# Branch and output stage of a hybrid encoder layer joined into one block, with the first output inputs split in the last branch tile

## What is computed

```python
y_gla  = o.astype(x.dtype) @ gla_wo                 # 512 -> 1024
y_pool = (pooled * jax.nn.silu(pool_z)) @ pool_wo
y_gdn  = o.astype(x.dtype) @ gdn_wo
gts = jax.nn.sigmoid(gates.astype(f32)).reshape(B, L, N_BRANCH, D_MODEL)
merged = gts[:, :, 0] * y_gla + gts[:, :, 1] * y_pool + gts[:, :, 2] * y_gdn
y = merged.astype(x.dtype) @ w_out
x = x + rmsnorm(y, norm_post)
```

## Time and profile before

| | us |
|---|---|
| median of three runs | 2622.28 |
| profiled execution | 2621.7 |
| span of the profiled execution (first to last instruction) | 2619.9 |
| PE busy | 2499.7 (95%) |
| DVE busy | 1036.3 (40%) |
| POOL busy | 808.8 (31%) |
| ACT busy | 675.5 (26%) |

### The profile page before, as it was taken

One profiled execution on the slowest core, in us unless ns is written; L12 is line 12 of the kernel. 1 busy time (PEld: TensorE's weight loads), 2 busy tenths in 40 slices (PEclk: granted clock), 3 DMA queues, 4 the chain that ended last, 5 costly groups with the idle time before them and its releaser, 6 DMA issues. The chain is left out here.

```text
span 2619.9 us, 40153 instructions
## 1 busy us (share of the span) xinstructions
PE 2499.7 (95%) x15943; PEld 2396.5 (91%) x15943; DVE 1036.3 (40%) x1603; ACT 675.5 (26%) x1350; POOL 808.8 (31%) x711
## 2 busy tenths in 40 slices
PE   5899999999999998998999999999999979997998
PEld 4799999999988898998999999999999879997886
DVE  6510011222455654002555555455555443323332
ACT  7111111111145431111232223222332243212222
POOL 1111121111111111114465456454555214332222
PEclk9899999999999999998999999999999879999999
DMA  5112412100111121242223324443224355543343
GB/s 159 47 66 107 193 63 74 66 33 33 66 50 49 49 74 68 74 136 68 82 76 111 111 81 127 159 122 97 81 78 108 119 174 179 198 162 140 114 145 106
DMA packets 200143, 264.95 MB, mean 101 GB/s; under 512 B 16176, under 2 KB 175296, under 8 KB 194432
## 3 DMA queue, kind: packets, MB, share of 16 engines
q1 hardware_dynamic: 200064, 263.86, 31.2%
HBM read 164.54 MB, written 99.29 MB: 101 GB/s over the span
## 5 line engine op out<-in xcount | busy, mean ns | idle before, releaser
L178 POOL TENSOR_TENSOR w_hi<-w_raw,zero 128x1024 fp32r<-128x1024 f32 x77 | 146.9, 1908 | 1243.0 <-PE dense L426 943.3
L424 PE MATMUL dense<-h_hi_first,w_hi 128*128 128x352 f32 x1080 | 355.2, 329 | 15.5 <-ACT row_y L671 8.4
L425 PE MATMUL dense<-h_lo_first,w_hi 128*128 128x352 f32 x1080 | 352.2, 326 | 0.0
L426 PE MATMUL dense<-h_hi_first,w_lo 128*128 128x352 f32 x1080 | 351.7, 326 | 0.0
L425 PE MATMUL dense<-h_lo_second,w_hi 128*128 128x352 f32 x1080 | 349.8, 324 | 0.0
L426 PE MATMUL dense<-h_hi_second,w_lo 128*128 128x352 f32 x1080 | 348.7, 323 | 0.0
L424 PE MATMUL dense<-h_hi_second,w_hi 128*128 128x352 f32 x1080 | 347.7, 322 | 0.0
L1314 PE MATMUL gate_bank<-h_hi_first,w_hi 128*128 128x352 f32 x768 | 274.4, 357 | 5.1 <-SPq L1232 4.4
L1314 PE MATMUL gate_bank<-h_hi_first,w_lo 128*128 128x352 f32 x768 | 249.5, 325 | 0.0
L1314 PE MATMUL gate_bank<-h_lo_first,w_hi 128*128 128x352 f32 x768 | 249.3, 325 | 0.0
L424 PEld LDWEIGHTS dense<-h_hi_first,w_hi 128*128 128x128 f32 x1080 | 206.1, 191 | 19.9 <-ACT row_y L671 8.7
(11 more groups left out here) (212 smaller groups left out, 4625.4 us busy)
## 6 DMA issues: line engine op xcount, KB each, us to landing
w_raw<-in_w_in SPq DMA_DIRECT2D x77, 512.0 KB, 5.8
rows_then_inputs<-scratch_feat SPq DMA_DIRECT2D x16, 1856.0 KB, 9.2
scratch_feat<-row_y SPq DMA_DIRECT2D x28, 1056.0 KB, 4.9
gate<-scratch_gates SPq DMA_DIRECT2D x12, 2112.0 KB, 8.7
scratch_gates<-gate_row SPq DMA_DIRECT2D x96, 176.0 KB, 1.9
o_raw<-scratch_branch_out SPq DMA_DIRECT2D x6, 2112.0 KB, 12.9
scratch_merged<-merged SPq DMA_DIRECT2D x48, 176.0 KB, 1.8
rows_then_inputs<-in_x_prompt SPq DMA_DIRECT2D x16, 512.0 KB, 3.7
```

Source lines behind the costliest of these rows:

```text
L178: nc.gpsimd.tensor_tensor(self.hi[:, p], raw, zeros, ALU.add).then_inc(self.high_ready, 1)
L424: nc.tensor.matmul(out, w_hi[:, p, k], h_hi[:, k, cols], start=(k == 0), stop=False)
L425: nc.tensor.matmul(out, w_hi[:, p, k], h_lo[:, k, cols], start=False, stop=False)
L426: mm = nc.tensor.matmul(out, w_lo[:, p, k], h_hi[:, k, cols], start=False, stop=(k == KD - 1))
```

## The change

`branch_phase` and `output_phase` become one function, `closing_phase`, with one block. What each engine did in the output stage follows in its queue directly on what it did in the branch stage, without the clearing of semaphores and the barrier between them. What is computed is the same, with the same operations.

Buffers: since the buffers of both stages don't fit side by side, those of the output stage lie over ones of the branch stage. The split w_out, the split and the raw merged tiles, x, the scaled result and so on are placed over `wo_hi` and `wo_lo`, over the gates (half 0) and over the ring and `o_raw` of `LateWeights`. `block_under(row)` tells which block m of wo must be through on PE before a row of 4096 bytes may be written. In PSUM the even token tiles have two banks of their own, `y_tok`, and the odd ones take two banks of the first buffer of `y`.

Order: in the last branch tile, SP loads the last row of w_out behind the store of block 3, waits for the stores 0 to 3 of that tile to land and loads merged 0 and 1; the gain is loaded behind the store of block 7, then x 0 and 1 when PE is through with the branch stage. ACT, behind the last gates, loads the table and makes the high rows of w_out and then those of merged 0 and 1, each when its block of wo is through: blocks 0, 1, 1, 2, 3, 3, 4, 5 for the rows, 5 and 6 for merged. DVE makes the low rows between its products: row 0 behind product 1, rows 1 and 2 behind product 2, row 3 behind 3, rows 4 and 5 behind 4, row 6 behind 5, row 7 and merged 0 behind 6, merged 1 behind 7. PE goes on from the last branch block to the first token tile.

```diff
...
+        w_hi = over("wout_hi", hi_at, [P, KD, DM], F32R)
+        w_lo = over("wout_lo", lo_at, [P, KD, DM], F32R)
+        m_hi = over("m_hi", hi_at + KD * ROW, [P, 2, KD, P], F32R)
+        m_lo = over("m_lo", lo_at + KD * ROW, [P, 2, KD, P], F32R)
+        x_in = over("x_again", hi_at + (KD + 2) * ROW, [P, 2, DM])
+        normed = over("normed", lo_at + (KD + 2) * ROW, [P, 2, DM])
+        w_last = over("wout_last", late.gate_at, [P, DM])
+        m_raw = over("m_raw", late.gate_at + ROW, [P, 2, KD, P])
+        gain = over("post_gain", late.ring_at, [P, DM])
+        squares = over("y_squares", late.ring_at + ROW, [P, DM])
+        result = over("result", late.o_at, [P, 2, DM])
...
+        y_tok = ctx.enter_context(nc.psum_tensor("y_tok", [P, DM], F32))
...
+        def tokens_bank(p):
+            return y[:, 0, 0:2, :].rearrange("p a b -> p (a b)") if p else y_tok
...
+        def block_under(row):
+            return ((row + 1) * ROW - 1) // (4 * K * P)
...
+                    sp.dma_start(y_out, result[0:n, p]).then_inc(stored[p], 16)
                 tile(0, first=True)
                 sp.wait_ge(wo_split, KD)
                 late.load_first(sp, d)
-                with sp.Fori(1, TILES_B - 1) as t:
+                with sp.Fori(1, LAST) as t:
                     tile(t)
                 sp.wait_ge(o_split, TILES_B * 3)
                 late.load_then(sp, d)
-                tile(TILES_B - 1, ahead=False)
+                for m in range(KD):
+                    store_merged(LAST, m)
+                    if m == 3:
+                        sp.dma_start(w_last[:, :], d["w_out"][(KD - 1) * P:KD * P, :]).then_inc(w_last_landed, 16)
+                        for q in range(2):
+                            sp.wait_ge(merged_stored[q], 16 * (4 * LAST + 2))
+                        load_m(0, 0)
+                        load_m(1, 1)
+                sp.wait_ge(w_split, late.FIRST)
+                sp.dma_start(gain[:, :], d["norm_post"].to_broadcast([P, DM])).then_inc(gain_landed, 16)
+                sp.wait_ge(y_ready, TILES_B * KD)
+                load_x(0, 0)
+                load_x(1, 1)
                 for q in range(2):
                     sp.wait_ge(merged_stored[q], 16 * 4 * TILES_B)
+                with sp.Fori(0, CHUNKS // 2 - 1) as i:
+                    for p in range(2):
+                        load_next_m(i * 2 + (p + 2), p)
+                        store(i * 2 + p, p)
+                        load_x(i * 2 + (p + 2), p)
+                load_next_m(CHUNKS, 0, NS_)
+                store(CHUNKS - 2, 0)
+                load_x(CHUNKS, 0, NS_)
+                store(CHUNKS - 1, 1)
+                store(CHUNKS, 0, NS_)
+                sp.wait_ge(stored[0], 16 * (CHUNKS // 2 + 1))
...
+                def w_row(k):
+                    act.wait_ge(y_ready, LAST * KD + block_under(k) + 1)
+                    if k == 0:
+                        act.wait_ge(late.first_landed, 16)
+                    if k == late.FIRST:
+                        act.wait_ge(late.then_landed, 16)
+                    if k == KD - 1:
+                        act.wait_ge(w_last_landed, 16)
+                    nc.scalar.copy(w_hi[:, k], w_raw(k)).then_inc(w_high, 1)
+                def high(t, i, p, n):
+                    act.wait_ge(m_landed[p], i * 16 + 16)
+                    if isinstance(t, int) and t < 2:
+                        act.wait_ge(y_ready, LAST * KD + block_under(KD + t) + 1)
+                    else:
+                        act.wait_ge(tok_ready, t - 1)
+                    nc.scalar.copy(m_hi[:, p, :, 0:n], m_raw[:, p, :, 0:n]).then_inc(m_high, 1)
...
+                    open_gates(LAST, half)
+                use_log_exp_tables(nc)
+                for k in range(KD):
+                    w_row(k)
+                act.wait_ge(eps_set, 1)
+                high(0, 0, 0, P)
+                high(1, 0, 1, P)
+                for p in range(2):
+                    statistics(p, p, P)
+                    high(p + 2, 1, p, P)
+                with act.Fori(1, CHUNKS // 2 - 1) as i:
+                    for p in range(2):
+                        statistics(i * 2 + p, p, P)
...
+                def token_tile(t, p, n):
+                    pe.wait_ge(m_split, t + 1)
+                    if isinstance(t, int) and t == 1:
+                        pe.wait_ge(y_gated, TILES_B * KD - 1)
+                    elif not (isinstance(t, int) and t < 2):
+                        pe.wait_ge(normed_ready, t - 1)
+                    for half in range(2):
+                        cols = slice(half * 512, half * 512 + 512)
+                        out = tokens_bank(p)[0:n, cols]
+                        for k in range(KD):
+                            if isinstance(t, int) and t == 0 and half == 0:
+                                pe.wait_ge(w_split, k + 1)
+                            nc.tensor.matmul(out, m_hi[:, p, k, 0:n], w_hi[:, k, cols], start=(k == 0), stop=False)
+                            nc.tensor.matmul(out, m_hi[:, p, k, 0:n], w_lo[:, k, cols], start=False, stop=False)
+                            mm = nc.tensor.matmul(out, m_lo[:, p, k, 0:n], w_hi[:, k, cols], start=False,
+                                                  stop=(k == KD - 1))
+                    mm.then_inc(tok_ready, 1)
                 tile(0, first=True)
                 with pe.Fori(1, TILES_B) as t:
                     tile(t)
+                token_tile(0, 0, P)
+                token_tile(1, 1, P)
+                token_tile(2, 0, P)
+                token_tile(3, 1, P)
+                with pe.Fori(1, CHUNKS // 4) as i:
+                    for u in range(4):
+                        token_tile(i * 4 + u, u % 2, P)
...
+                for m in range(KD):
+                    gated(LAST, m)
+                    for k in range(KD):
+                        if block_under(k) == m - 1:
+                            w_row_low(k)
+                    if block_under(KD) == m - 1:
+                        m_low(0, 0, P)
+                m_low(1, 1, P)
+                dve.wait_ge(gain_landed, 16)
+                norm(0, 0, P)
+                m_low(2, 0, P)
+                norm(1, 1, P)
+                m_low(3, 1, P)
+                with dve.Fori(1, CHUNKS // 2 - 1) as i:
+                    for p in range(2):
+                        norm(i * 2 + p, p, P)
+                        m_low(i * 2 + (p + 2), p, P)
+                norm(CHUNKS - 2, 0, P)
...
```

More of the change, by code:

```diff
@@ L1925, in store, with tile @@
                         .then_inc(merged_stored[m % 2], 16)
-                def tile(t, ahead=True, first=False):
+                def tile(t, first=False):
                     if first:
@@ L2051, in _ @@
-                low(0, 0)
-                weights_low(0)
-                low(0, 1)
-                low(0, 2)
-                weights_low(1)
-                for m in range(KD - 1):
-                    if m + 2 < KD:
-                        weights_low(m + 2)
-                    gated(0, m, first=True)
-                low(1, 0)
-                low(1, 1)
-                gated(0, KD - 1)
-                low(1, 2)
-                with dve.Fori(1, TILES_B - 1) as t:
-                    tile(t)
@@ L2066, in _ @@
-                tile(TILES_B - 1, ahead=False)
-            @block.gpsimd
-            def _(pool):
-                def tile(t, first=False):
-                    for m in range(KD):
-                        q = m % 2
-                        pool.wait_ge(y_gated, t * KD + (m + 1))
-                        nc.gpsimd.tensor_tensor(part[:, q], prod[:, q, 0], prod[:, q, 1],
-                                                ALU.add).then_inc(part_ready, 1)
-                        pool.wait_ge(part_ready, t * KD + (m + 1))
-                        if not (first and m < 2):
-                            pool.wait_ge(merged_stored[q], t * (4 * 16) + (m // 2) * 16)
-                        nc.gpsimd.tensor_tensor(merged[:, q], part[:, q], prod[:, q, 2],
-                                                ALU.add).then_inc(merged_ready, 1)
-                tile(0, first=True)
-                with pool.Fori(1, TILES_B) as t:
-                    tile(t)
@@ L2298, in _, with tile, token_tile @@
             def _(pool):
-                def tile(t, i, p, n):
+                def tile(t, first=False):
+                    for m in range(KD):
+                        q = m % 2
+                        pool.wait_ge(y_gated, t * KD + (m + 1))
+                        nc.gpsimd.tensor_tensor(part[:, q], prod[:, q, 0], prod[:, q, 1],
+                                                ALU.add).then_inc(part_ready, 1)
+                        pool.wait_ge(part_ready, t * KD + (m + 1))
+                        if not (first and m < 2):
+                            pool.wait_ge(merged_stored[q], t * (4 * 16) + (m // 2) * 16)
+                        nc.gpsimd.tensor_tensor(merged[:, q], part[:, q], prod[:, q, 2],
```

(12 more changed lines are left out.)

289 lines of the change are left out of this document (102 added, 187 removed).

## The result

The changed kernel takes **2604.78 us** (median of four runs, 2602.7 to 2609.2) where the kernel before took 2622.01 in runs beside it: a ratio of 0.9936 with a 95% interval of 0.9919 to 0.9954. A second series of five runs gave 2603.79 (2602.6 to 2604.4) against 2620.73, a ratio of 0.9933 (0.9919 to 0.9946). The forecast was 2605.2 with a range of 2603.0 to 2609.5. The profiled execution took 2605.52 with a span of 2603.7 (forecast 2604.6 and 2602.8).

The account below looks back on a forecast made before the run. PE was taken to bound both stages, with one hole between them. Removing 17.57 us and adding a 0.45 us wait gave 17.1 us less, from a median of 2622.28 to 2605.2 us, range 2603.0 to 2609.5.

Parts of the forecast that it names:

- The hole: Between branch and output stage: PE's idle time and the stretched first token tile go, next tile starting 17.57 us earlier.
- The new wait: Last branch tile, before block 4: PE waits for product 2, queued behind low row 0; +0.45 us, bounds zero and 2.4.
- The cover at the end of the last tile: Merged 0's low part done at 2405.0, wanted by PE at 2406.93: 1.9 us cover, cost nothing, upper bound 2.1 us.
- Rival 1: First token tile: lock or late landing delays merged 0's low part; 0.8 to 2.1 us, 2606 to 2609; chance 0.10.
- The next tiles: Later token tiles: merged 2 issued near 2413.6, split by about 2424, wanted at 2428.7; cover 4.7 us, cost nothing.
- rivals 2 and 4: Third token tile's inputs late, 2608.8, chance 0.04; merged loads delaying every third tile, level or slower (2627.7), chance 0.08.
- The tail: End of the kernel: clearing more semaphores taken at nothing, bounds nothing and 0.95 us.
- Rival 3: ACT and DVE order keeps the split behind the branch stage; some 10 us of gain left, 2612; chance 0.02.
- The other signs: Around the boundary: last product near 2407.1, squares near 2418.0, clock 1.00 between 2400 and 2435, no first token matmul wait.

Follow-up runs that it names:

- The join alone: Kernel before with both stages in one block but nothing of merged 0 or w_out split ahead: 2621.28 us, ratio 0.9999.
- the two late variants: Changed kernel with merged 0 and 1 loaded and split only after the branch stage: 2619.50 us; or with w_out's low rows after the last product: 2612.15 us.
- the move the other way: Changed kernel with DVE making w_out's low row 0 one product earlier, ACT making the high row no earlier: 2612.72 us.

## Why the prediction was right

**The hole (17.57 us).** Measured without the wait of the next point it is 28.45 - 10.91 = 17.54. Both of its parts, the 14.17 us of standing and the 3.2 us by which the first tile was stretched, are gone. The number is right, but the prediction's reason for the second part is not: it says that the first tile took 14.12 us because the clock had fallen. In the trace of before the clock was back at full by about 2425, and PE waited for DVE's rows again behind that. The last row ends at 2428.62, and PE begins with it there; the 21 matmuls up to it take 7.86 us in place of 4.79, which is 3.1 of the 3.2 us. Since the change takes the low clock and the rows away together, the wrong cause did the sum no harm. That is luck.

```profile
2424.80:2435.00 10.20, 9.86 (x41) 7.21 (x40) 4.95 (x5) 2.00 (x3) 0.00 (x0) 0.99 0.06 15
...
2428.67 0.50 PE L2237 MATMUL y_tok<-wout_hi,m_hi 128*128 128x512 f32 x1 [0.16 <-DVE wout_lo L2280]
```

The join alone shows that the boundary proper is 0.90 of the 17.54 (the prediction worked out 0.95 from the store's landing), and the two late variants show that the rest had to be taken away on both chains.

**The new wait (+0.45, bounds 0 and 2.4).** It is there, at the forecast place: product 2 was to run from 2382.5 to 2383.8, and with the whole trace 0.6 us later it runs from 2383.00 to 2384.25. Its size is (0.34 + 0.26) - 2 x 0.16 = 0.28 us in one profile and 0.43 in the other. That its chain was read rightly (second gates, table, high row 0, low row 0, product) is shown by two different moves, of DVE's row and of the table load (in one profile each), which each remove it, and by the move the other way, which makes it 6.14 us. The prediction let product 3 catch the lateness up. It didn't: it ended at 2388.44, 1.7 us ahead of PE's block 5 at 2390.14, as low rows 1 and 2 took 3.10 us beside POOL's adds and not 2.4. Product 4 was the first that waited for PE again.

**The cover at the end of the last tile (1.9 us).** Right in sign, too large: merged 0's low part ends at 2404.08 + 1.97 = 2406.05 for a start at 2407.30, 1.25 us ahead. The mis-sized step is the subtraction at 1.23 us. Its 1.97 comes from POOL's adds, which stretch in turn (to 1.86 at most in this tile, where the prediction said 2); the timeline of POOL:

```profile
2403.11 1.85 POOL L2302 TENSOR_TENSOR part<-prod 128x352 f32<-128x352 f32 x1 [2.83 <-DVE prod L2219]
2405.13 1.73 POOL L2307 TENSOR_TENSOR merged<-part,prod 128x352 f32<-128x352 f32 x1 [0.16 <-POOL part L2302]
```

The rows fit each other as turns: row 7 runs on DVE until 2404.17, the add until 2404.96, merged 0's low part until 2406.05, the second add until 2406.86. This is what the Trainium skill (SBUF — State Buffer, section Who interferes with whom) says of the shared port pair, that it is an exclusive lock. There, holding it for a whole instruction is said of VectorE's two-port modes, and of a subtraction with both inputs in SBUF only that it contends; in this trace the subtraction, too, starts when the add lets go and takes about its own length from there (1.09 us). By that reading one short add can push the subtraction by what is left of it, here 0.8 us, and not by the 2 us of the raw 3.21. Rival 1 was thus priced too high at its upper end, and the rule was the better guide. The loads were later than said as well: SP issued merged 0 at 2393.3 in place of 2392.4. Of this, 0.6 is the shift of the whole trace, and the rest goes with product 3, which was late as told above. ACT had merged 0 rounded by 2400.5, still 3.6 us before DVE asked for it.

**The next tiles.** Merged 2 was issued at 2413.97 (2413.6 was said) and split by 2425.9 for a need at 2429.1. That is 3.2 us of cover in place of 4.7, again by a subtraction beside a POOL add (2.69 us in place of 1.23). Nothing was lost: tiles 1 to 16 take 174.24 us in every kernel of this study, so rivals 2 and 4 did not come.

**The tail (taken at nothing, bounds 0 and 0.95).** It took 0.52 us more, within the bounds but wrong as a value. 0.29 of it is POOL's last add, which starts 3.89 us behind the squares in both kernels with two blocks and 4.17 to 4.19 in all eight joined ones. The 0.29 lie wholly between the end of DVE's last scaling and the add (0.18 and 0.47 us). The rest lies behind the issue of the last store, which took 3.1 us to land in place of 2.9; but in the join alone it took 2.9, and the end still came 0.5 us later. 12 more semaphores gave 0.10. Why the last add starts later, and what stands at the end, stays open.

**Rival 3** was put at 2612, for DVE's rows all behind the last product. The run with the low rows late is the nearest to it and gave 2612.15, but not by its working: merged 0 was split ahead there, so PE started at 2409.26 and not at 2410.8, and the rows then paced it more slowly. That the two numbers agree is chance.

In sum: 17.1 us were forecast and 16.2 are in the profiles. Of the 0.9 us between them, 0.52 is the tail and 0.35 the scatter ahead of the branch stage. The branch stage is longer by 0.47, about the 0.45 put there, but only 0.28 of that is the new wait, and from product 1 to the last product it is 0.20; the agreement is chance. So is part of that of the medians, 17.2 and 16.9 us apart in the two series for a forecast of 17.1: the tail that was taken at nothing is less than their scatter. The other signs that the prediction named came: the last product at 2407.50 (2407.1 said), the squares at 2418.41 (2418.0), a clock of 1.00, and no wait at the first or third token tile. Ahead of 2360 us the trace moved by 0.35 to 0.6 us, which the scatter of the start covers.

## What to carry to other kernels

Where the bound engine stands at a boundary between stages, follow the chain to its head: the wait is named after its last link, and two chains that both end at the restart (here a read-back and a split) have to be taken ahead together, since taking only one gave back 3.3 or 10.1 of 17.5 us, the 0.9 of the join included. Don't put work behind a stop down to a low clock before looking at what else paces it: in the kernel before it was the rows. When such work is put into an in-order queue between pieces that the bound engine needs, place it by when its input can be there, not by when its buffer is free: one subtraction placed a product too early cost 8 to 9 us, and one placed a product later cost nothing. Write down the cover of each hidden piece; most were right here, and those that were too large had a VectorE subtraction beside a GpSimd add.

## What the runs showed of the hardware

A single stop of TensorE of 2.48 us in otherwise full work left its granted clock at 1.00 and cost 2.75 us. Stops of 2.57, 0.85 and 0.22 us with light work between them took it to 0.50 for some 6 to 7 us (0.79, 0.50 and 0.81 over stretches of 3, 4 and 4 us). One stop of 6.14 us took it to 0.50 from some 2 us into the stop (0.60 over the 6 us from 2377) until 2388.4, some 6 us of work behind it. So the length of the stop alone doesn't decide, since the one of 2.48 us passed. Each of these is one profile.

What the low clock costs hangs on what paces the engine behind the stop. Where all inputs were there it cost 2.9 us (21 branch matmuls of 0.29 us in place of 0.16, behind 6.14 us of standing) and 1.9 us (nine token matmuls of 0.43 in place of 0.23, behind 12.20 us). Where the engine had to wait for the split rows of w_out anyway, in the kernel before and with the low rows late, it cost next to nothing: in both PE began with the last row within 0.1 us of the row's end.

Where a VectorE subtraction with both inputs in SBUF met a GpSimd add, their durations fit turns: a subtraction of 1.22 us took 1.97 beside an add of 0.95 and 2.69 beside one of 2.39, and adds of 0.95 took 1.73 to 1.86. Beside a product, which has one input in PSUM, neither was stretched (1.26 us for a product and 0.96 for the add that overlapped it).
